# Latent attention: values of two steps multiplied together behind every second step's scores

## What is computed

```
def mla_attend(q_nope, q_rope, k_nope, k_rope, v):
    s = (einsum('bqhd,bkhd->bhqk', q_nope, k_nope)
         + einsum('bqhr,bkr->bhqk', q_rope, k_rope)) * MLA_SCALE
    p = jax.nn.softmax(s, axis=-1)
    return jnp.einsum('bhqk,bkhd->bqhd', p, v)
```

## Time and profile before

| | |
|---|---|
| Time, median of three runs | 2534.51 us (2534.51, 2535.52, 2528.3) |
| Span of the profiled execution | 2530.5 us |
| Busy in the span | PE 92%, PEld 68%, DVE 60%, ACT 47%, POOL 15% |
| Latent attention in the span | about 1762 to 2046 us |

### The profile page before, as it was taken

The page is one execution under the profiler, slowest core; times in us unless marked ns, Lnnn a source line. Parts: engine busy times, 40 slices in busy tenths (PEclk is TensorE's granted clock), DMA queues, the critical chain, the costliest instruction groups (busy, mean ns, idle before and its releaser), DMA issues.

```text
span 2530.5 us, 27448 instructions
## 1 busy us (share of the span) xinstructions
PE 2328.4 (92%) x11068; PEld 1719.4 (68%) x11068; DVE 1529.0 (60%) x1877; ACT 1187.9 (47%) x1669; POOL 373.4 (15%) x258
## 2 busy tenths in 40 slices
PE   6988789798699999999989999898999998899998
PEld 5766555475488888888768676554555467778876
DVE  5766157544799999999771024746555647533475
ACT  3255256521388888888662044425444432312231
POOL 2000012000111111111100000011555534000014
PEclk9999899898899999999989998998999999899999
DMA  3201010116899999999751010010000032111141
GB/s 118 67 31 37 0 67 1 67 75 256 347 372 379 384 379 404 391 393 380 273 184 46 1 51 1 1 38 1 1 1 34 17 125 75 37 66 50 44 161 53
DMA packets 98874, 342.08 MB, mean 135 GB/s; under 512 B 21276, under 2 KB 46661, under 8 KB 71096
## 3 DMA queue, kind: packets, MB, share of 16 engines
q1 hardware_dynamic: 87096, 318.76, 33.6%
q0 software_dynamic: 10448, 17.28, 1.8%
q10 hardware_dynamic: 1200, 4.24, 0.4%
HBM read 323.41 MB, written 33.60 MB: 141 GB/s over the span
## 4 chain that ended last, share of the span: by engine, by line
PE 81%; DVE 9%; ACT 5%; DMA 2%; issue 2%; SPq 0%; DVEq 0%; POOL 0%; ACTq 0%; POOLq 0%
PE psm L230 78%; DVE mem L953 1%; PE psm L1722 1%; ACT mem L1143 1%; DMA mem<-in_ada_w_dram 1%; PE psm L1073 1%; DVE r L337 1%; DMA mem<-in_w_in_dram 1%; DVE mem L2741 1%; PE psm L1745 1%; PE psm L464 1%; ACT mem L1109 1%; DMA mem<-in_odd_w_out_dram 1%; DVE small L3008 0%; DVE r L3264 0%
## 5 line engine op out<-in xcount | busy, mean ns | idle before, releaser
L230 PE MATMUL psm<-r,r 128*128 128x512 f32 (+4 forms) x7438 | 1777.5, 397 | 76.4 <-DVE r L337 17.9
L230 PEld LDWEIGHTS psm<-r,r 128*128 128x128 f32 (+3 forms) x7438 | 1380.6, 189 | 472.0 <-issue 63.7
L337 DVE TENSOR_TENSOR r<-mem,r 128x1024 fp32r<-128x1024 f32 x448 | 525.8, 1221 | 174.7 <-ACT r L328 169.5
L328 ACT ACTIVATE r<-mem 128x1024 fp32r<-128x1024 f32 x448 | 441.1, 1052 | 33.5 <-DMA mem<-in_w_in_dram 22.1
L230 PE MATMUL psm<-mem 128*64 128x128 f32 (+13 forms) x2230 | 358.8, 437 | 34.7 <-ACT mem L816 9.1
L230 PEld LDWEIGHTS psm<-mem 128*64 128x64 f32 (+6 forms) x2230 | 167.9, 163 | 155.7 <-issue 88.7
L3216 POOL TENSOR_TENSOR mem<-mem 128x1024 f32<-128x1024 f32 x63 | 153.9, 2443 | 177.6 <-ACT mem L3171 176.9
L3171 ACT ACTIVATE mem<-psm 128x512 f32<-128x512 f32 x160 | 95.4, 597 | 148.5 <-PE psm L230 141.1
L3008 DVE TENSOR_REDUCE small<-psm 128x1 f32<-128x1280 f32 x64 | 95.2, 1488 | 104.6 <-PE psm L230 104.2
L230 PE MATMUL psm<-mem,cst 128*128 128x512 f32 (+4 forms) x274 | 115.1, 638 | 23.3 <-ACT mem L924 5.5
L265 ACT ACTIVATE small<-small 128x1 f32<-128x1 f32 (+3 forms) x26 | 7.7, 295 | 236.1 <-DVE small L374 151.0
(11 more groups left out here) (338 smaller groups left out, 1774.7 us busy)
## 6 DMA issues: line engine op xcount, KB each, us to landing
mem<-in_exp_w_gate_dram SPq DMA_DIRECT2D x64, 1024.0 KB, 7.4
mem<-in_exp_w_up_dram SPq DMA_DIRECT2D x64, 1024.0 KB, 7.6
mem<-in_exp_w_down_dram SPq DMA_DIRECT2D x64, 1024.0 KB, 7.3
mem<-in_ada_w_dram SPq DMA_DIRECT2D x16, 1024.0 KB, 14.0
mem<-in_odd_w_in_dram SPq DMA_DIRECT2D x10, 1024.0 KB, 5.3
mem<-in_even_w_in_dram SPq DMA_DIRECT2D x9, 1024.0 KB, 5.3
mem<-in_x_dram SPq DMA_DIRECT2D x16, 512.0 KB, 7.1
mem<-in_w_in_dram SPq DMA_DIRECT2D x8, 1024.0 KB, 5.3
```

The source lines that it names most:

```text
L230: return p.e.matmul(o, l, r, start=start, stop=stop, skip_group_check=True)
L328: p.e.activation(h, mem(kb + 8, [R * n])[:, w * q:w * q + w], ACT.Copy).then_inc(*self.hi_done.up(i, q))
L337: p.e.tensor_tensor(l, mem(kb + 8, [R * n])[:, w * q:w * q + w], h.bitcast(F32), SUB).then_inc(*self.lo_done.up(i, q))
```

## The change

PE's queue, which had V of step t - 2 behind every step's scores and items, now has V of the steps t - 3 and t - 2 behind the scores and items of the odd steps, and nothing behind those of the even steps. The sums on PE also stand in odd steps alone: those after a last digit 4 stay three steps late, those after a last digit 9 are now four steps late. The division, on ACT and DVE, moves from four to five steps late, so from the odd steps 13, 23, 33 ... to the even steps 14, 24, 34 ... No instruction is added or removed.

```
@@ latent_tensor
                 if t < 80:
                     scores_of_pair(p, t)
                     beside_tensor(p, t)
-                if 0 <= t - 2 < 80:
-                    values_tensor(p, t - 2)
-                if 0 <= t - 3 < 80 and STEPS[t - 3][2] in (4, 9):
-                    sums_tensor(p, t - 3)
+                if t % 2:
+                    for k in (t - 3, t - 2):
+                        if 0 <= k < 80:
+                            values_tensor(p, k)
+                    for k in (t - 4, t - 3):
+                        if 0 <= k < 80 and STEPS[k][2] in (4, 9):
+                            sums_tensor(p, k)
@@ latent_scalar
-                if 0 <= t - 4 < 80 and STEPS[t - 4][2] == 9:
-                    hp, half, i = STEPS[t - 4]
-                    p.wait_ge(*ml_pe.at("sum", t - 4))
+                if 0 <= t - 5 < 80 and STEPS[t - 5][2] == 9:
+                    hp, half, i = STEPS[t - 5]
+                    p.wait_ge(*ml_pe.at("sum", t - 5))
@@ latent_vector
-                if 0 <= t - 4 < 80 and STEPS[t - 4][2] == 9:
-                    hp, half, i = STEPS[t - 4]
+                if 0 <= t - 5 < 80 and STEPS[t - 5][2] == 9:
+                    hp, half, i = STEPS[t - 5]
                     y = YM[:, hp, 512 * half:512 * half + 512]
-                    p.wait_ge(*ml_pe.at("pv", t - 4))
+                    p.wait_ge(*ml_pe.at("pv", t - 5))
```

## The result

Seven runs of each kernel: 2519.74 us after (2517.17 to 2520.65) against 2533.12 before (2525.31 to 2537.91). The ratio is 0.9948 with a 95% interval of 0.9936 to 0.9961, so the change takes 13.4 us off. The forecast was 2521.2 us, 13.3 off.

What follows compares the result with a forecast made beforehand. PE's order was taken as the bound, with 17.3 us lost at items 25, 45 and 65. The terms +2.3 - 1.1 - 0.8 - 0.4 - 13.3 + 0 gave -13.3 us, so 2521.2 us, range 2509 to 2536.

Steps and rivals of the forecast that it cites:

- Part 2: Odd step's item on PE waits 0.33 us for DVE's reduction; 26 pairs each 0.09 longer, +2.3 us.
- Part 3: Pairs without an odd item: seven with digits 8 and 9 save 1.1 us, the last five 0.8.
- Step 70: A second V group ahead of its scores covers their 0.43 us wait: -0.4 us.
- Part 4: Division a step later on ACT and DVE: losses at items 25 and 45 go, -13.3 us; 65 taken as 0.
- Part 1: Fewer changes between scores with items and V on PE: 0.35 us per pair, 14 over 40, if nothing ends later.
- The first rival: Odd item on PE is not held: -9.1 us in place of +2.3, giving 2509.8 us; chance 0.10.
- Step 65: Loss near item 65 stays, about 3.4 us and some clock against 3.94: taken as 0, bounds -3.9 to +4.
- The sign that the prediction named: On PE near step 66, a wait of 1 us or more would be left.
- The start: First two pairs with two items: V is missing there anyway, so no cost was counted for them.
- new waits over 1 us for L3008 elsewhere: On PE, such waits for DVE's reduction were to show the division's forecast wrong.
- The second rival: Collision of DVE and POOL only moves elsewhere: sum within ±5 us of zero, 2534.5 us; chance 0.26.
- The third: Short holds at odd items lower PE's clock: kernel slower, 2547 us with 12 of 26 pairs hit; chance 0.12.

Runs made afterwards that it cites:

- e10: Against the kernel after the change: V of step 0 put back behind step 2; 2517.4 us in a single run, no ratio.
- e4: Against the kernel after the change: DVE's reduction of an item split into two instructions, bank 5 first, then banks 6 and 7; 2509.5 us, ratio 0.9913.
- e9: Against the kernel before: division a step later and reduction in two instructions, V still one group behind every step; 2517.0 us, ratio 0.9938.
- e6: Against e4: V of step 0 put back behind step 2; 2507.5 us, ratio to the kernel before 0.9911.
- e1: Against the kernel before: only the division moved from four to five steps late, on ACT and DVE; 2516.3 us, ratio 0.9941.
- e8: Against the kernel before: only DVE's half of the division a step later, ACT's Ln and Exp unmoved; 2516.0 us, ratio 0.9946.
- e2: Against the kernel before: only V in pairs behind the odd steps, sums and division unmoved; 2522.9 us, ratio 0.9963.
- e3: Against the kernel after the change: item of even steps with last digit under 8 put between the two heads' scores; 2519.8 us, ratio 0.9954.
- e5: Against the kernel before: only DVE's reduction of an item split into two instructions; 2532.1 us, ratio 1.0004.
- e7: Against e6: roundings for post0 and DVE's remainders spread over steps 50 to 58 instead of 60 to 65; 2505.7 us, ratio to before 0.9900.

## Why the prediction was right, step by step

| Term | forecast us | measured us | from |
|---|---|---|---|
| Part 2, held item, 26 pairs | +2.3 (0.09 each) | +2.9 (0.11) | 6.47 against 6.36 |
| Start, V of step 0 moved | none | +0.85 | 12.26 against 11.42; e10 |
| Part 3, digits 8 and 9 | -1.1 | -1.1 | 1792.62 - 1786.16 = 6.46 against 6.62 |
| Part 3, last five pairs | -0.8 | -0.6 | 5.11 against 5.22 |
| Step 70 | -0.4 | about -0.5 | the wait is gone |
| Part 4, 25 and 45 | -13.3 | -13.3 | no wait over a pair's own |
| Part 4, 65 | 0 (-3.9 to +4) | -3.0 | 1991.45 - 1983.20 = 8.25 against 7.32 |
| Sum | -13.3 | -14.8 | the stage: -14.9 |

**Part 1** was right in size: a change of width costs 0.35 there and back, and e4 gets 0.33 of it per pair. e9 against e6 shows it in the time. The prediction put beside it the rule on draining of the Trainium skill, TensorEngine Tiling (Array Packing), Key Properties, as the case of the whole 14 us for 40 pairs. The runs show a price for the change of width and 9 to 10 us in all: only 26 pairs could save the 0.33, the other 12 save 0.16 or 0.11.

**Part 2** was right in mechanism: the odd item is held by the reduction, as the earlier trace rows showed for item 1. e4 takes the hold away and 0.44 per pair come back. The first rival (the item is not held) is ruled out by the waits of all pairs.

**Part 4** was right in its result, and e1 and e8 show that it alone makes the gain. But the text gave two grounds, the division's place and the two V groups behind the odd step, as if both were needed ("it isn't late, since two V groups lie between"). e1 has no pairs and e2 no moved division, and both clear the steps 25 and 45 (e2 all but 0.6 us each). Only at 65 they differ by more.

**Step 65** was the term that was mis-sized. "The split after it comes 0.1 behind a POOL addition, waits it out" was decided by 0.1 us in a sum of some ten terms, and it went the other way. All engines near step 66 of the kernel after:

```profile
1985.28 1.22 DVE L3261 TENSOR_TENSOR r<-mem,r 128x1024 fp32r<-128x1024 f32 x1
...
1985.75 2.98 POOL L3219 TENSOR_TENSOR mem<-mem 128x1024 f32<-128x1024 f32 x1 [4.21 <-ACT mem L3174]
```

The split started at 1985.28, POOL's addition at 1985.75; it was POOL that then took 2.98 in place of 2.4. The bounds of -3.9 to +4 held it. The sign that the prediction named, a wait of 1 us or more near step 66, did not come: the waits there are 0.55 and 0.30.

**The start** was missed altogether. The text said of the first two pairs that V is missing there anyway. That is so for step 1, but V of step 0 stood behind step 2 and covered item 3, and the change takes it away. Item 3's wait of 1.05 is, by the letter, one of the "new waits over 1 us for L3008 elsewhere" that were to show Part 4 wrong; it has nothing to do with the division, since e2, where the division has not moved, has the same 1.05.

**Luck.** The time came out 0.1 us from the forecast, closer than the working deserves. The stage lost 14.9 us where 13.3 were forecast, since 65 gave 3.0 that the sum had at 0 and the start and the held items took back 1.4; and what follows the stage, which the forecast left unchanged, is 1.5 longer.

The second rival, that the collision only moves, is what e2 shows at 65 and e3 behind each division. The third, that short holds pull the clock down, didn't come: 26 holds with 0.17 of PE's modelled idle time each left it at 1.00 in every stretch of 20 us. The Trainium skill, TensorEngine Tiling (Array Packing), PSUM Bottleneck, warns that emptying PSUM may become the bottleneck once TensorE is faster. The trace agrees in kind: DVE's reduction out of PSUM holds PE, at 0.44 us per pair (6.47 against e4's 6.03).

In one line: the division's move alone takes 16.2 us off the stage (e1), and the merging of V, which the change is about and which is worth -10 us where nothing holds PE, adds 1.3 on top of it (267.2 to 268.5; the terms give 2.9 + 0.85 - 1.1 - 0.6 - 0.5 = +1.6), because the held item eats it. Counted the other way round, the pairs alone take 10.6 off (e2, 283.4 to 272.8), since they too give DVE its time at 25 and 45, and the division's move the last 4.3. So the shares of the two edits depend on which is counted first. The price of merging itself is shown by e4, e6 and e9, where no collision is left at 25 and 45; that the order on DVE suffices is shown by e1 and e8.

## What to carry to other kernels

When a reordering makes one engine's work contiguous, look at what the pieces in between were covering; here a 1.49 us reduction over three banks had 2.4 us of values and scores to finish in before the next item, and then only the 1.4 of the scores. Splitting it so that the first bank comes free early paid 9 to 10 us more (e4), and nothing in the kernel before (e5). An instruction that waits for another engine's result should stand behind, not ahead of, work on its queue that is ready and needed soon: the place of two multiplications on DVE was worth as much as the whole change. Take a wait's price with what the clock does afterwards.

## What was not expected of the hardware

How long a wait is doesn't alone tell whether the granted clock falls after it. Item 3 of the kernel after waits 1.05 us and V behind it keeps its 1.87, at a granted clock of 1.00; in e4 waits of 1.08 and 0.36, with one matmul between them, are followed by 3.61, at 0.50. In e5 1.79 and 0.37 were followed by the lower level as 2.59 was in the kernel before. So shortening a wait from 2.59 to 1.79 bought next to nothing (0.5 us of the stage), and e4, with a second wait of 0.36 behind one of 1.08, takes 2.0 us more up to step 4 than the changed kernel (14.26 against 12.26). What exactly decides it, no run here separates.

What follows the stage is 1.5 us longer in the kernel after. Busy time in the stretch from 120 to 240 us behind the stage's end, first of the kernel before, then after (timeline stretch, busy time of PE, PEld, DVE, ACT and POOL, granted clock, share and rate of the transfers):

```profile
2165.34:2285.34 120.00, 110.39 (x481) 90.80 (x480) 45.51 (x115) 29.09 (x42) 0.00 (x0) 0.94 0.15 50
```

```profile
2148.64:2268.64 120.00, 109.37 (x472) 89.92 (x471) 45.59 (x115) 28.56 (x41) 0.00 (x0) 0.93 0.16 50
```

The granted clock is 0.94 and 0.93 there. e1, e8, e9 and e7 have 484.9 to 485.2 us after their stages and e2, e3, e4, e6 and e10 486.2 to 486.9, like the changed kernel (486.7, before 485.2). The code there is the same in all. Whether the pairs cause it stays open, since e7 has them and is short, and e5 hasn't and has 486.0. The part ahead of the stage, which is also the same in all, ends between 1760.11 and 1765.35, so 1.5 us is not more than such parts vary by themselves.
